# Up projections of three networks as seven block products, with weight sums made partly by accumulating transfers

## The chip, the cores and the metric

One core of a Trainium2 chip runs the whole program. The time is device microseconds of one launch; before the change the median of three runs is 2175.71 us (2175.65 to 2176.05).

## The reference

Two transformer blocks follow each other on 512 tokens of width 1024, all in float32. Block one has a mixer (forgetting attention beside gated linear attention), a cross attention, and an MLP. Block two has a gated network (ffn1), a token mixer, a second gated network (ffn2) and a final norm. What the change touches is the three networks:

```python
# block one
u = relu(rms_norm(h, norm_mlp_g) @ mlp_w1)        # 1024 -> 4096
h = h + (u * u) @ mlp_w2                          # 4096 -> 1024
# block two, twice (ffn1 and ffn2)
n = rmsnorm(x, g)
x = x + 0.5 * ((silu(n @ w1) * (n @ w3)) @ w2)    # 1024 -> 2816 twice, 2816 -> 1024
```

## The kernel before, in words

Activations lie with the features across the 128 partitions: `h` is 8 tiles (k) of 128 features by 512 tokens. Every float32 operand of a matrix product is split into a high part of the type that TensorE multiplies (fp32r) and a low part, the remainder. A product is then three matmuls, high by high, high by low and low by high (`product`, L557 to L559), added in one PSUM bank.

Weights come in panels of 1024 rows by 256 columns. SP issues their load into one of two `raw` buffers (`load`, L432, which waits on `conv_done`, so until VectorE has converted the panel before); ScalarE copies a panel to `wh` (`conv` of its block, L1365), VectorE subtracts to `wl` (`conv`, L2114), and TensorE runs it in `panel_t`: for each of the two 128-column halves c, 8 tiles k by 3 matmuls of 512 tokens, 48 in all, into the bank `lin0` or `lin1`. A down panel over six k tiles has 36. `begin(p, c)` makes TensorE wait until VectorE has emptied that bank of the panel before, and `pe.wait_ge(conv_done, p + 1)` until the panel is converted. Each engine works through its own instructions in the written order.

A network is cut into chunks. A chunk has its up panels first and then four down panels whose result VectorE adds to `h` (`residual`). The MLP has four chunks of 4 up and 4 down panels. ffn1 and ffn2 have two chunks of 8 up panels (w1 and w3 in turns) and 4 down, then one of 6 up panels and 4 down panels of six k tiles. The up products are made from the features without the token's norm factor; VectorE multiplies the factor `N_rs` in afterwards. The MLP does VectorE relu by factor, ScalarE square and high part, VectorE low part. The gated one (`gated`) does VectorE factor, ScalarE silu, VectorE factor and product, ScalarE high part, VectorE low part. The results stand in `ah`, `al` (in `xh`, `xl` for ffn2), from where `panel_t` takes them as the k tiles of the down panels.

GpSimd has no work beyond the start. The sub-blocks outside the networks keep their code.

Of the kernel before, what the change touches and what calls it, by code (L numbers as in the profile page):

```python
# [11 lines left out]
PART = 128  # L12
# [26 lines left out]
for name_, count_ in (("small", 1), ("fqk", 4), ("fv", 2), ("gqk", 2), ("gv", 2), ("gr", 2), ("xk", 4), ("xv", 4),  # L39
                      ("wout", 4), ("xq", 4), ("xo", 4), ("mlp", 32), ("ffn1", 34),  # L40
                      ("mix2", 32), ("mnsa", 8), ("wout2", 4), ("ffn2", 34)):
    P0[name_] = at
    at += count_
# [59 lines left out]
MLP0 = {"mlp": 2, "ffn1": 2 + 32, "ffn2": 2 + 32 + 22}  # L103
ML_S0 = MLP0["ffn1"]

# [69 lines left out]
def build(nc, d, out):  # L175
    ctx = ExitStack()
    with ctx:
# [8 lines left out]
        xh = sb("xh", [PART, KT, T], F32R)  # L186
        xl = sb("xl", [PART, KT, T], F32R)
        ah = sb("ah", [PART, KT, T], F32R)
        al = sb("al", [PART, KT, T], F32R)
        raw = sb("raw", [PART, 2, KT, PC])  # L190
# [19 lines left out]
        AW = 16360  # L210
# [55 lines left out]
        sm_done, sm_z = sem("sm_done"), sem("sm_z")  # L266
# [26 lines left out]
        e_half, e_add, e_sq, e_ac = sem("e_half"), sem("e_add"), sem("e_sq"), sem("e_ac")  # L293
        out_c = [sem("out_c" + str(t)) for t in range(QT)]
# [59 lines left out]
        E_t, E_u = A(2, T), A(2, T)  # L354
# [45 lines left out]
        def landed(p):  # L400

            return 16 * (p // 2 + 1)

# [4 lines left out]
        def _(sp):  # L408
# [60 lines left out]
            for r in range(0, D_FF // D):  # L469
                for j in range(4):  # L470
                    load(r * 8 + (P0["mlp"] + j), (P0["mlp"] + j) % 2, mw1[:, :, bass.ds(r * D + j * PC, PC)])
                for j in range(4):
                    load(r * 8 + (P0["mlp"] + 4 + j), (P0["mlp"] + j) % 2, mw2[:, bass.ds(r * KT, KT), j * PC:(j + 1) * PC])

            def ffn(name):
                w1, w3, w2 = ffw[name]
                p0 = P0[name]
                for r in range(0, 2):
                    for j in range(4):
                        for e, w in enumerate((w1, w3)):  # L480
                            load(r * 12 + (p0 + 2 * j + e), (p0 + e) % 2, w[:, :, bass.ds(r * D + j * PC, PC)])
                    for j in range(4):
                        load(r * 12 + (p0 + 8 + j), (p0 + j) % 2, w2[:, bass.ds(r * KT, KT), j * PC:(j + 1) * PC])
                for j in range(3):
                    for e, w in enumerate((w1, w3)):
                        load(p0 + 24 + 2 * j + e, (p0 + e) % 2, w[:, :, 2 * D + j * PC:2 * D + (j + 1) * PC])
# [2598 lines left out]
```

## Time and profile before

| | before |
|---|---|
| median of three runs | 2175.71 us |
| span of the profiled execution | 2174.4 us |
| TensorE busy | 2157.7 us, 99% |
| VectorE busy | 1144.9 us, 53% |
| ScalarE busy | 904.4 us, 42% |
| GpSimd busy | 0.2 us |
| transferred | 199.45 MB, mean 92 GB/s |

The span runs from the first to the last instruction of one profiled execution; the result gives no separate device time for that execution, so the median of the runs stands for it, 1.3 us above the span. "Busy" counts the time in which at least one instruction of an engine runs. Matmuls are pipelined and their ends are modelled: the distance between the starts of two neighbours says what one costs, not its duration.

### The profile page before, as it was taken

To read this page: it belongs to the slowest core of one execution; us is meant where nothing else is said; L and a number is where in the kernel's file an instruction comes from. 1 tells how busy PE (TensorE), PEld (TensorE's weight loads), DVE (VectorE), ACT (ScalarE), POOL (GpSimd) and SP (SyncE) were. 2 spreads that over 40 slices of the span, in tenths; PEclk is the share of its full clock that TensorE was granted. 3 is DMA by queue.
4 is the path that set the end of the run, shared out by engine and by line. 5 is a ranking of instruction groups with operands and counts; after the bars stand their busy time and mean duration, and the time that the engine had idled before them with its cause. 6 is when DMAs were issued, how large, how long until landed. Compare 5 with 4: busy or idle time off the path is not lost.

```text
span 2174.4 us, 28238 instructions
## 1 busy us (share of the span) xinstructions
PE 2157.7 (99%) x11510; PEld 1777.1 (82%) x11510; DVE 1144.9 (53%) x1985; ACT 904.4 (42%) x1526; POOL 0.2 (0%) x4
## 2 busy tenths in 40 slices
PE   9999999999999999999999999999999999999999
PEld 7888988888888888888888878887777888888887
DVE  4754664453433454344357677647776455434345
ACT  6654545442322332222234465546666233222224
POOL 0000000000000000000000000000000000000000
PEclk9999999999999999999999999999999999999999
DMA  5121521133333223323223622321111333333321
GB/s 186 59 78 59 194 97 59 59 95 99 97 94 99 94 90 98 104 87 107 86 90 95 199 80 82 98 83 49 45 30 40 97 97 97 98 97 97 98 87 68
DMA packets 190194, 199.45 MB, mean 92 GB/s; under 512 B 7777, under 2 KB 185074, under 8 KB 189554
## 3 DMA queue, kind: packets, MB, share of 16 engines
q1 hardware_dynamic: 190066, 197.66, 29.0%
q8 instruction: 91, 1.49, 0.3%
q14 instruction: 37, 0.30, 0.0%
HBM read 188.73 MB, written 2.10 MB: 88 GB/s over the span
## 4 chain that ended last, share of the span: by engine, by line
PE 97%; DVE 1%; ACT 1%; issue 1%; DMA 0%; SPq 0%; DVEq 0%; ACTq 0%
PE lin L557 28%; PE lin L559 27%; PE lin L558 27%; PE turned L658 3%; PE score L753 3%; PE mix L767 2%; PE mix L1201 1%; PE mix L1040 1%; PE score L1020 1%; PE score L869 1%; PE score L1252 0%; PE mix L1260 0%; PE score L1004 0%; PE mix L777 0%; DMA raw<-in_w_in_dram 0%
## 5 line engine op out<-in xcount | busy, mean ns | idle before, releaser
L557 PE MATMUL lin<-xh,wh 128*128 128x512 f32 (+1 forms) x1478 | 581.4, 393 | 1.7 <-DVE wl L2120 1.2
L559 PE MATMUL lin<-xh,wl 128*128 128x512 f32 (+1 forms) x1478 | 568.7, 385 | 0.0
L558 PE MATMUL lin<-xl,wh 128*128 128x512 f32 (+1 forms) x1478 | 567.6, 384 | 0.0
L557 PE MATMUL lin<-ah,wh 128*128 128x512 f32 x1044 | 407.8, 391 | 0.5 <-DVE h L2173 0.5
L559 PE MATMUL lin<-ah,wl 128*128 128x512 f32 x1044 | 405.5, 388 | 0.0
L558 PE MATMUL lin<-al,wh 128*128 128x512 f32 x1044 | 405.4, 388 | 0.0
L2114 DVE TENSOR_TENSOR wl<-raw,wh 128x2048 fp32r<-128x2048 f32 x129 | 295.7, 2292 | 185.1 <-ACT wh L1365 185.1
L1365 ACT ACTIVATE wh<-raw 128x2048 fp32r<-128x2048 f32 x129 | 245.8, 1906 | 263.6 <-PE lin L559 263.6
L557 PEld LDWEIGHTS lin<-xh,wh 128*128 128x128 f32 x1478 | 277.9, 188 | 63.1 <-issue 9.9
L559 PEld LDWEIGHTS lin<-xh,wl 128*128 128x128 f32 x1478 | 277.7, 188 | 56.5
L558 PEld LDWEIGHTS lin<-xl,wh 128*128 128x128 f32 x1478 | 278.2, 188 | 52.4 <-issue 1.0
L557 PEld LDWEIGHTS lin<-ah,wh 128*128 128x128 f32 x1044 | 196.0, 188 | 41.6 <-issue 0.9
L559 PEld LDWEIGHTS lin<-ah,wl 128*128 128x128 f32 x1044 | 196.0, 188 | 40.6
L558 PEld LDWEIGHTS lin<-al,wh 128*128 128x128 f32 x1044 | 196.1, 188 | 40.3 <-issue 0.2
L2120 DVE TENSOR_TENSOR wl<-raw,wh 128x1024 fp32r<-128x1024 f32 x90 | 109.6, 1221 | 40.2 <-ACT wh L1372 39.7
L2226 DVE CUSTOM_DVE_ANT_0 arena<-score,cst 128x128 f32<-128x128 f32 (+2 forms) x224 | 97.6, 487 | 57.9 <-PE score L753 46.7
L1462 ACT ACTIVATE arena<-arena,negm 128x128 f32<-128x128 f32 (+2 forms) x224 | 122.9, 555 | 3.0 <-DVE negm L2226 3.0
L2156 DVE TENSOR_TENSOR arena<-lin,N_rs 128x512 f32<-128x512 f32 x66 | 45.5, 689 | 139.5 <-PE lin L559 139.4
L1450 ACT ACTIVATE arena<-turned 128x512 f32<-128x512 f32 (+1 forms) x128 | 68.9, 582 | 112.4 <-PE turned L658 112.1
L1372 ACT ACTIVATE wh<-raw 128x1024 fp32r<-128x1024 f32 x90 | 94.2, 1053 | 35.6 <-PE lin L559 23.6
L1822 ACT ACTIVATE arena<-arena 128x512 f32<-128x512 f32 x44 | 27.8, 633 | 170.9 <-DVE arena L2156 170.9
L557 PE MATMUL lin<-wh,xh 128*128 128x256 f32 x320 | 92.5, 289 | 0.0
(349 smaller groups left out, 2120.8 us busy)
## 6 DMA issues: line engine op xcount, KB each, us to landing
raw<-in_ffn_w_dram SPq DMA_DIRECT2D x60, 1024.0 KB, 5.3
raw<-in_w_in_dram SPq DMA_DIRECT2D x38, 1024.0 KB, 5.3
raw<-in_mlp_w_dram SPq DMA_DIRECT2D x32, 1024.0 KB, 5.4
raw<-in_xattn_wkv_dram SPq DMA_DIRECT2D x8, 1024.0 KB, 5.5
raw<-in_w_out_dram SPq DMA_DIRECT2D x8, 1024.0 KB, 5.1
arena<-arena SPq DMA_DIRECT2D x104, 64.0 KB, 2.0
raw<-in_ffn_w_dram SPq DMA_DIRECT2D x8, 768.0 KB, 4.6
raw<-in_xattn_wq_dram SPq DMA_DIRECT2D x4, 1024.0 KB, 5.3
```

What stands on the lines that cost most here:

```text
L557: nc.tensor.matmul(o, w[0], x[0], start=first, stop=False)
L558: nc.tensor.matmul(o, w[0], x[1], start=False, stop=False)
L559: return nc.tensor.matmul(o, w[1], x[0], start=False, stop=last)
L658: mm = nc.tensor.transpose(pt[a][:, to:to + PART], PB[:, j % 2, a, lo:lo + PART], ident)
L753: mm = nc.tensor.matmul(ps[a][:, col:col + nk], q(piece, a, slice(t * PART, nk)), k(piece, a, nk), start=True, stop=True)
L1365: nc.scalar.activation(wh[:, p % 2], raw[:, p % 2], ACT.Copy).then_inc(hi_done, 1)
L1372: nc.scalar.activation(wh[:, p % 2, :, cols], raw[:, p % 2, :, cols], ACT.Copy).then_inc(hi_half[c], 1)
L1450: op = nc.scalar.activation(PTs[:, a, 0:w], pt[a][:, 0:w], ACT.Copy)
L1462: op = nc.scalar.activation(PB[:, s % 2, a, col:col + nk], SM[:, a, col:col + nk], ACT.Exp, bias=negm[:, at:at + 1], scale=-1.0, accum_out ...
L2114: nc.vector.tensor_tensor(wl[:, p % 2], raw[:, p % 2], wh[:, p % 2].bitcast(F32), ALU.subtract).then_inc(conv_done, 1)
L2120: nc.vector.tensor_tensor(wl[:, p % 2, :, cols], raw[:, p % 2, :, cols], wh[:, p % 2, :, cols].bitcast(F32), ALU.subtract).then_inc(conv_d ...
L2226: op = nc.vector.tensor_tensor_reduce(out=SM[:, a, col:col + nk], in0=ps[a][:, col:col + nk], in1=mask, scale=scale, scalar=BIG, op0=ALU.a ...
```

## The change

A 2 by 2 block product by the Strassen-Winograd scheme replaces the plain one in all chunks but one of each network. For a pair of weight panels (`one`, `two`; in the gated networks w1 and w3 of the same columns) the weight blocks are A11, A12 (the upper and the lower four k tiles of `one`) and A21, A22 (those of `two`), each 4 tiles of 256 columns. The token blocks are the two halves of 256 tokens. Such a pair is a group: seven products (`PRODUCTS`), each of 2 by 4 by 3 = 24 matmuls of 256 tokens. The MLP has three phases of two groups, ffn1 and ffn2 two phases of four groups each, 22 groups in all, each phase followed by its four down panels as before.

Weight blocks: SP loads A21, A11, A12, A22 of a group, 512 KB each, into a buffer set: `raw`, or one that lies in `xl` (`al` for ffn2), in turns. S1 is A21 + A22: GpSimd issues a transfer that adds A22 from HBM to the loaded A21 (`add_22`). S2 = S1 + A11 and S4 = A12 + S2 are made by VectorE (`sum_2`, `sum_4`). S3 = A11 + A21 is again an adding transfer (`add_21`), issued once `sum_2` is done. Each of the seven blocks is converted by ScalarE and VectorE (`block_high`, `block_low`) into one of six slots (four half panels of `wh`, `wl`, two in `xh` or `ah`).

Token blocks: seven parts (`XS_h`, `XS_l`), made once per network, now with the norm factor multiplied in. They are made during the first chunk (`token_parts`, `token_parts_high`, `token_parts_low`), one quarter m at a time: in the gated networks quarters 0 and 1 behind its second and third pair of up panels, 2 and 3 between its down tiles. The chunk of 6 up panels and 36-matmul down panels now comes first instead of last.

Results: products share three PSUM banks per group. ScalarE copies a partial result out three times (`kept`) and VectorE adds or subtracts (`made_11`, `made_22`, `made_21`); the nonlinearity then runs on these tiles. Some semaphores at the end of the program are merged, and GpSimd's descriptor area is set to 2048.

The core of the diff:

```diff
+PRODUCTS = [(A11, B11, 0), (A12, B21, 2), (S2, T2, 0), (S3, T3, 1), (S1, T1, 0), (A22, T4, 1), (S4, B22, 0)]
...
+            def group_loads(g, p, free):
+
+                one, two = weights(g)
+                before = same_buffers(g)
+                for b, src in ((BZ, two[:, 0:HT]), (BP, one[:, 0:HT]), (BQ, one[:, HT:KT]), (BR, two[:, HT:KT])):
+                    if before:
+                        q = before[-1]
+                        if b == BZ:
+                            sp.wait_ge(st_a, sum_count(q, 2))
+                        else:
+                            sp.wait_ge(st_l, high_count(q, {BP: S3, BQ: S4, BR: A22}[b]))
+                    if buffers(g):
+                        sp.wait_ge(lin_done, 2 * free)
+                    else:
+                        sp.wait_ge(conv_done, p - 1 + b // 2)
+                    sp.dma_start(raw_of(g, b), src).then_inc((st_r, st_z, st_r, st_r)[b][buffers(g)], 16)
...
+            def add_21(g):
+
+                pool.wait_ge(st_a, sum_count(g, 1))
+                if g:
+                    pool.wait_ge(st_p, 16 * g)
+                pool.dma_start(raw_of(g, BP), weights(g)[1][:, 0:HT], accum_op=ALU.add).then_inc(st_p, 16)
...
+            def group(g):
+
+                (net, r), i = PHASE_OF[g]
+                for n, (a, b, at) in enumerate(PRODUCTS):
+                    o = banks(g)[at].rearrange("p (f n) -> p f n", f=2)
+                    (left_h, left_l) = parts_of(g, a)
+                    pe.wait_ge(st_l, high_count(g, a))
...
+                    if n in (2, 4, 5):
+                        pe.wait_ge(st_e, 3 * g + {2: 1, 4: 2, 5: 3}[n])
+                    elif n == 6:
+                        pe.wait_ge(st_c, 3 * g + 2)
+                    for c in range(2):
+                        cols = slice(c * PART, (c + 1) * PART)
+                        for k in range(HT):
+                            begins = n in (0, 1, 3) and c == 0 and k == 0
+                            nc.tensor.matmul(o[:, c, :], left_h[:, k, cols], XS_h[:, b, k, :], start=begins, stop=False, skip_group_check=True)
...
# scalar: a gated phase
+                for g in range(g0, g0 + n):
+                    more = g + 1 < g0 + n
+                    if g > g0:
+                        finish(g - 1)
+                    block_high(g, S3)
+                    if g > g0:
+                        high(g - 1, RIGHT, E_ur, gate_count(g, 0))
+                    kept(g, 0, (ml_e, 2 * MLP_G + gate_count(g, -1)))
+                    block_high(g, S4)
+                    if more:
+                        block_high(g + 1, A11)
+                    act.wait_ge(st_c, 3 * g + 1)
+                    nc.scalar.activation(E_tl, E_tl, ACT.Silu).then_inc(ml_s, 1)
+                    kept(g, 1, (ml_lo, made_count(g, -1)))
+                    if more:
+                        block_high(g + 1, A12)
+                    else:
+                        conv(p)
+                    kept(g, 2, (ml_lo, made_count(g, 0)))
+                    if more:
+                        block_high(g + 1, S1)
+                        block_high(g + 1, S2)
+                        block_high(g + 1, A22)
# vector: the token parts, a gated phase, the first chunk
+            def token_parts(name, gain, m):
+
+                if m:
+                    dve.wait_ge(st_l, part_count(name, m, 0))
+                for e in range(2):
+                    k = m + HT * e
+                    op = nc.vector.scalar_tensor_tensor(P_F[:, e, :], h[:, k, :], gcol(gain, k), N_rs[:], ALU.mult, ALU.mult)
+                op.then_inc(st_a, 1)
+                dve.wait_ge(st_a, token_count(name, m, 1))
+                nc.vector.tensor_tensor(P_T[:, T3 - T1, :], P_F[:, 0, RIGHT], P_F[:, 1, RIGHT], ALU.subtract).then_inc(st_a, 1)
...
+            def token_parts_low(name, m):
+
+                dve.wait_ge(st_h, part_count(name, m, 3))
+                low(XS_l[:, B11, m, :], P_F[:, 0, LEFT], XS_h[:, B11, m, :], st_l)
...
+                for g in range(g0, g0 + n):
+                    more = g + 1 < g0 + n
+                    if g > g0:
+                        finish(g - 1)
+                    block_low(g, S3)
+                    if g > g0:
+                        low_part(g - 1, RIGHT, E_ur, made_count(g, 0))
+                    block_low(g, S4)
+                    made_11(g)
+                    if more:
+                        block_low(g + 1, A11)
+                        block_low(g + 1, A12)
+                        block_low(g + 1, S1)
+                        sum_2(g + 1)
+                    else:
+                        conv(p)
+                    made_22(g)
+                    if more:
+                        block_low(g + 1, S2)
+                        sum_4(g + 1)
+                        block_low(g + 1, A22)
+                    made_21(g)
+                    gate(g, E_ul, E_tl, 3, gate_count(g, 1))
...
+                first = 4 if name == "mlp" else 5
+                residual(p, None, None, scale, 2, {0: third, 1: fourth, 2: fifth, first: early, first + 1: later})
+                last()
...
+                for j in range(TAIL):
+                    gated(p0 + 2 * j, m0 + 2 * j, j, dst, (lambda: token_parts_low(name, j - 2)) if j == 2 else None)
+                    if j:
+                        token_parts(name, own, j - 1)
+                token_parts_low(name, 1)
+                chunk(name, own, p0 + 6, 0.5)
+                ffn_phase(name, 1, dst)
+                rest(name, 2, 0.5)
+                ffn_phase(name, 2, dst)
+                residual(p0 + 14, after, gain, 0.5, 3 if after == "mix2" else 4)
```

`finish(g)` is, on ScalarE, the silu of `E_tr` and the high part of `E_ul`, on VectorE the low part of `E_ul` and the product of `E_ur` by `E_tr`. `third` is `token_parts` of quarter 2, `fourth` `token_parts_low` 2 and `token_parts` 3, `fifth` `token_parts_low` 3; `early` is the low parts of A11 and A12, `later` those of S1 and S2 with `sum_2` and `sum_4`, `last` that of A22. `token_parts` has two multiplications over 512 elements and four additions over 256, the first three in a chain; `token_parts_low` three subtractions over 256, 512 and 1024 elements. The MLP's phases are alike, with more instructions for square and parts; there the down panels' k tiles 4 to 7 wait for the last group (in ffn1 and ffn2 tiles 6 and 7).

In `residual` the pieces of `between[k]` stand behind the add of down tile k and ahead of the `conv` that follows tiles 1 and 3. ScalarE's order there is: high parts of token quarter 2, `conv` of the third down panel, high parts of quarter 3, `conv` of the fourth, and then the blocks A11, A12, S1, S2, A22 of the phase's first group, of which A11 waits until all of A11, A12 and A22 have landed. The blocks S3 and A22 of a first group go into slots that come free when the last down panel ends.

## Rows read from the trace of the kernel before

**Rows 1.** The page, parts 1 and 4: engine shares, and the chain that ended last.

```profile
PE 2157.7 (99%) x11510; PEld 1777.1 (82%) x11510; DVE 1144.9 (53%) x1985; ACT 904.4 (42%) x1526; POOL 0.2 (0%) x4
PE 97%; DVE 1%; ACT 1%; issue 1%; DMA 0%; SPq 0%; DVEq 0%; ACTq 0%
```

**Rows 2.** MLP, ffn1, ffn2: length, busy PE, PEld, DVE, ACT, POOL, clock, DMA, GB/s.

```profile
448.00:797.00 349.00, 349.00 (x1538) 288.43 (x1538) 151.22 (x144) 111.01 (x115) 0.00 (x0) 1.00 0.31 97
797.00:1164.00 367.00, 366.79 (x1619) 303.02 (x1618) 168.02 (x166) 105.11 (x100) 0.00 (x0) 1.00 0.29 93
1807.00:2161.00 354.00, 353.94 (x1562) 292.84 (x1563) 155.56 (x151) 99.69 (x94) 0.00 (x0) 1.00 0.28 89
```

**Rows 3.** Timeline of PE, first and last 512-token matmul of the MLP (1536).

```profile
448.40 0.79 PE L557 MATMUL lin<-xh,wh 128*128 128x512 f32 x1
...
796.78 0.39 PE L559 MATMUL lin<-xh,wl 128*128 128x512 f32 x1
```

**Rows 4.** Timeline of PE, a run of 264 matmuls of 256 columns, and its stretch.

```profile
235.06 0.36 PE L557 MATMUL lin<-xh,wh 128*128 128x256 f32 x1
...
266.69 0.28 PE L559 MATMUL lin<-wh,xl 128*128 128x256 f32 x1
235.06:266.70 31.64, 31.64 (x267) 1.00 0.69 233
```

**Rows 5.** Costliest groups by shape, VectorE: busy, mean ns of one.

```profile
L2114 DVE TENSOR_TENSOR wl<-raw,wh 128x2048 fp32r<-128x2048 f32 x129 | 295.7, 2292 | 185.1 <-ACT wh L1365 185.1
L2120 DVE TENSOR_TENSOR wl<-raw,wh 128x1024 fp32r<-128x1024 f32 x90 | 109.6, 1221 | 40.2 <-ACT wh L1372 39.7
L2138 DVE SCALAR_TENSOR_TENSOR xl<-h,gT,xh 128x512 fp32r<-128x512 f32 x40 | 29.6, 751 | 27.7 <-ACT xh L1401 27.7
L2125 DVE TENSOR_TENSOR xl<-arena,xh 128x512 fp32r<-128x512 f32 x30 | 20.2, 686 | 1.2
L2475 DVE TENSOR_TENSOR h<-mix,h 64x256 f32<-64x256 f32 x16 | 6.1, 417 | 0.2
L2242 DVE TENSOR_SCALAR arena<-arena,coef 128x512 f32<-128x512 f32 x32 | 14.1, 484 | 0.6
L2242 DVE TENSOR_SCALAR arena<-arena,coef 128x128 f32<-128x128 f32 x32 | 7.7, 284 | 0.6
```

**Rows 6.** The same view for ScalarE.

```profile
L1365 ACT ACTIVATE wh<-raw 128x2048 fp32r<-128x2048 f32 x129 | 245.8, 1906 | 263.6 <-PE lin L559 263.6
L1372 ACT ACTIVATE wh<-raw 128x1024 fp32r<-128x1024 f32 x90 | 94.2, 1053 | 35.6 <-PE lin L559 23.6 <-DMA raw<-in_xattn_wkv_dram 4.5 <-DMA raw<-in_cmp_w_dram 3.7
L1812 ACT ACTIVATE ah<-arena 128x512 fp32r<-128x512 f32 x32 | 20.2, 632 | 1.0
L1383 ACT ACTIVATE arena<-lin 128x512 f32<-128x512 f32 x40 | 23.7, 592 | 42.2 <-PE lin L559 42.1
L1460 ACT ACTIVATE arena<-arena 128x256 f32<-128x256 f32 x8 | 3.1, 413 | 2.5 <-DVE arena L2936 2.5
```

**Rows 7.** Timelines of PE and DVE where ffn1's last down panels begin.

```profile
1122.07 0.39 PE L557 MATMUL lin<-ah,wh 128*128 128x512 f32 x1
...
1122.37 0.69 DVE L2640 TENSOR_TENSOR arena<-lin,arena 128x512 f32<-128x512 f32 x1 [4.75 <-PE lin L559]
...
1125.57 2.29 DVE L2114 TENSOR_TENSOR wl<-raw,wh 128x2048 fp32r<-128x2048 f32 x1 [1.11 <-ACT wh L1365]
1127.78 0.68 DVE L2175 SCALAR_TENSOR_TENSOR h<-lin,h 128x512 f32<-128x512 f32 x1
```

**Rows 8.** The page, part 6: transfers, KB each, median us to landing.

```profile
raw<-in_mlp_w_dram SPq DMA_DIRECT2D x32, 1024.0 KB, 5.4
...
raw<-in_ffn_w_dram SPq DMA_DIRECT2D x8, 768.0 KB, 4.6
...
h<-in_x_t_dram SPq DMA_DIRECT2D x2, 1024.0 KB, 9.2
```

**Rows 9.** Waits of PE between 448 and 1160 us: the whole answer.

```profile
PE turned L607 <- DVE arena L2133: 0.4, 2, 0.2
```

More of the change, by code:

```diff
@@ new lines, in phase, with made @@
+            def phase(name, r, Y, panels=4):
+                g0, n, p = PHASES[name, r]
+                for g in range(g0, g0 + n):
+                    group(g)
+                def made(k):
+                    if name == "mlp":
+                        pe.wait_ge(ml_lo, made_count(g0 + k // 4, 4))
+                    else:
+                        pe.wait_ge(ml_lo, made_count(g0 + k // 2, 2))
+                for j in range(panels):
+                    panel_t(p + j, (p + j) % 2, Y, each=made if j == 0 else None)
@@ L1102, in _ @@
+                phase(name, 1, Y)
+                phase(name, 2, Y, 3 if name == "ffn2" else 4)
             ffn("ffn1", X, Y)
@@ new lines, in chunk, with third, fourth, fifth @@
+            def chunk(name, gain, p, scale):
+                early, later, last = first_blocks(PHASES[name, 1][0])
+                def third():
+                    token_parts(name, gain, 2)
+                def fourth():
+                    token_parts_low(name, 2)
+                    token_parts(name, gain, 3)
+                def fifth():
+                    token_parts_low(name, 3)
+                first = 4 if name == "mlp" else 5
+                residual(p, None, None, scale, 2, {0: third, 1: fourth, 2: fifth, first: early, first + 1: later})
+                last()
@@ new lines, in rest @@
+            def rest(name, r, scale):
+                early, later, last = first_blocks(PHASES[name, r][0])
+                first = 4 if name == "mlp" else 5
+                residual(PHASES[name, r][2] - 4, None, None, scale, 2, {first: early, first + 1: later})
+                last()
+            chunk("mlp", "norm_mlp_g", p + 4, 1.0)
+            for r in range(1, D_FF // D):
+                if r > 1:
+                    rest("mlp", r, 1.0)
+                mlp_phase(r)
+            residual(p + 16, "ffn1", "ffn1_norm_2")
@@ L2630, in gated @@
+            def gated(p, m, j, dst, between=None):
                 for c in range(2):
                     scaled(p, c, E_t[:, c, :])
+                if between:
+                    between()
                 for c in range(2):
```

538 lines of the change are left out of this document (425 added, 113 removed).

## The prediction

> **What bounds the kernel now.** I read the shares of the engines and the chain of waits first: TensorE is busy 99% of the span, and 97% of the chain that ended last is TensorE [rows 1]. Then the stretches of the three networks, 1070 us together: TensorE has no idle time there at the full granted clock (1.00, the 2.4 GHz level), VectorE is busy 43 to 46% and ScalarE 28 to 32% [rows 2]; TensorE's own waits over the first two of them come to 0.4 us [rows 9]. So work taken from TensorE counts in full there, and anything else counts only where it makes TensorE wait. The profiled execution's span is 2174.4 us, 1.3 below the median; I work on the span and add 1.3.
>
> **What TensorE saves.** The 1536 matmuls of the MLP start 348.38 us apart from first to last: 0.2270 us each [rows 3]. A pair of panels has 96: 21.79 us. A group has 7 x 24 = 168 matmuls of 256 columns. A run of 264 such matmuls, bank changes included, takes 31.63 us for 263 steps: 0.1203 us [rows 4], more than half of 0.2270, since some 13 ns of each are fixed. So a group takes 20.20 us, and the gain is 1.58 us, 7%, not the eighth that seven for eight suggests. 22 groups: 34.8 us. The other panels are the same ones in another order: nothing.
>
> **What is late in a gated group.** VectorE has 7 low parts and 2 sums of 1024 elements at 1.22, and 7 operations of 512 at 0.69: 15.8 of 20.2 us; ScalarE 7 x 1.05 + 3 x 0.59 + 4 x 0.63 = 11.7 [rows 5, 6]. In the MLP it is 17.2 and 14.2. That fits, so what counts is order. I laid the written orders out by hand from the row durations. Two corrections come from rows: back to back on an engine the next operation starts 0.08 us before the recorded end (a 2.29 conversion hands over after 2.21), and VectorE starts on a finished tile 0.30 us after TensorE's next start [rows 7]. With T the start of a group, products end every 2.89 us. The copy behind product 4 ends at T+12.4, S1 is converted high to 13.4 and low to 14.7, `sum_2` ends at 15.9. Then `add_21` runs; call its time from `sum_2` to landing X. In the next group (20.2 later) ScalarE has silu, high part, S3's high part, another high part and `kept(g, 0)` in this order, and TensorE's third product at +5.8 waits for that copy. S3's high part must therefore begin by +3.6: no wait while X is under 8.0. Above it each of the 12 such transitions loses X - 8.0. The 3 in the MLP behave nearly alike. S3's low part, `made_22` (done at 16.7 for product 7 at 17.3) and `add_22` (about 29 us early) are in time.
>
> **X.** No row has an adding transfer or one issued by GpSimd. Lower bound: 768 KB lands in 4.6 and 1024 KB in 5.4, so 512 KB in about 3.8. Upper bound: twice the 1024 KB row, 10.8; the slowest 1024 KB row has 9.2 [rows 8]. An add reads both operands, 1024 KB, so that row is the nearest; I take 6.5, the middle of 3.8 and 9.2, since the issuing path is untested. Rate is no limit: a group moves 3 MB in 20.2 us, some 156 GB/s, and the stretch of rows 4 ran at 233 with 69% of the engines [rows 4].
>
> The Trainium skill (Collectives: The Full Stack, on why a reduce-scatter is half of an all-gather) says that an add in a transfer costs two source reads and not its arithmetic. By it X would be the 1024 KB row, 5.4, and the time some 3 us lower than my forecast; no trace here shows an add.
>
> **The ffn's first chunk.** Here I expect TensorE to lose. A quarter's `token_parts` takes 2 x 0.75 and 4 x 0.42, partly overlapped: 3.1 us; `token_parts_low` 0.4 + 0.7 + 1.2, less overlaps, 2.1 [rows 5]. In front of down tile 0 stand the last low parts, the conversion of a down panel (ends at +5.7 after the down panels begin, as the trace shows at that place [rows 7]), `token_parts` 1 (to 8.8), ScalarE's high part of 1024 (to 9.9) and `token_parts_low` 1 (to 12.0). The add of tile 0 ends at 12.7. A down panel of 36 matmuls is 36 x 0.227 = 8.17 us, and the second one's first half needs that bank at 8.2: 4.5 us lost. Then `token_parts` 2, the add of tile 1, `token_parts_low` 2, `token_parts` 3 and a conversion come before the add of tile 2, which ends 12.1 us after tile 0's, where TensorE wants it 8.17 after: 4.0 lost. Two networks: 17.0 us. In the MLP the same pieces stand in panels of 10.9 us, and the critical adds end 1.5 us or more ahead of need: nothing.
>
> **The first group of a phase.** A11's high part waits for all three plain loads, and the last two are issued when the last down panel is converted. Behind the short down panels (phase 1 of ffn1, ffn2) that is 4.8 us after the third panel's start; they land at 10.3, A11 and A12 follow, S1 is low at 15.5, `sum_2` ends 0.4 after the phase begins, where 5.8 is the third product's mark: 5.8 - 0.4 - 1.6 (S3's high part and the copy) = 3.8. Two phases lose X - 3.8 = 2.7 each: 5.4 us. Behind whole down panels `sum_2` ends 2.1 before the phase: X - 6.3 = 0.2, two of them 0.4. In the MLP S1 is made one tile earlier: nothing up to 9.7.
>
> **The end of a phase.** MLP: relu, high, square, high and a low part run in series behind the last product, ending at 3.4, and k tile 4 wants them at 4 x 0.68 = 2.7: 0.7 x 3 = 2.1 us. Gated: 4.1 against tile 6 at 4.1: nothing.
>
> **The sum.** 34.8 - 17.0 - 5.4 - 0.4 - 2.1 = 9.9 us. Span 2164.5, time 2165.8. The range of X alone: at 3.8, 15.7 less (2160); at 5.4, 2163; at 8.0, 2171.8; at 9.2, the 15 transitions and 4 phase starts bring 2194; at 10.8, about 2228.
>
> **Rivals.** (1) *All hidden*: VectorE's insertions don't reach TensorE, because my hand order has errors of a few us at a place that comes only four times. For it: VectorE is 46% busy [rows 2]. Against: its order is fixed, and 8.17 us are to hold 12.1 us of its work between the adds of tiles 0 and 2. The time: 2175.7 - 34.8 + 2 = 2143; half hidden, 2153. (2) *The adding transfer is slow*, X over 8.5. It decides from 8.0 on, since S3's high part stands in ScalarE's order ahead of `kept(g, 0)`. At 9.2, 2194. For it: GpSimd issues nothing now, and 512 rows of 1 KB in two reads have no row here. (3) *Narrow matmuls cost more in place*: groups break even at 21.79 / 168 = 0.1297 us; at 0.125 the gain is 17 us, and the time 2183. Against: the 264 of rows 4 ran at 0.1203 with a semaphore wait every 24.
>
> The Trainium skill has a rule that speaks for (2): SBUF — State Buffer, the box on VectorE blocking transfers, says that a VectorE instruction in a two-port mode locks GpSimd out of writing descriptors; it measured a transfer of 0.62 us stretched to 3.1. That would make X about 9.
>
> As a mechanism of this kernel it would lengthen each add by a VectorE instruction or two. The rows show a fast mode only in L2242, 200 ns for 384 elements more (0.52 ns each); the conversions take 1071 ns for 1024 more (1.05 ns) [rows 5], and the phases have only such operations and products of two tensors. I give it 5%, inside (2).
>
> **Chances.** Forecast, X of 3.8 to 8.0 with the losses as worked out: 50%. (1), whole or half: 18%. (2): 22%. (3): 5%. Other losses of 5 to 10 us beyond mine: 5%. A measurement tells 0.2%, 4.4 us, from no change: same is 2171.4 to 2180.1. Faster is the forecast but for its upper edge, and (1): 69%; same is that edge, the start of (2), and small extra losses: 12%; slower the rest of (2) and (3): 19%. Range 2147 to 2190: it leaves out the wholly hidden case and X above 9. The forecast's own range is 2159 to 2172.
>
> **What would show it.** Matmuls of 256 columns at 0.120; a group 20.2 us apart from the next; TensorE waits before the second and the third down panel of ffn1's and ffn2's first chunk, 4 to 5 us each, ended by VectorE's add; X read as the gap from `sum_2`'s end to S3's high part; waits at the third product of a phase, ended by `kept`; VectorE about 78% busy in gated phases. I am wrong if TensorE runs through the first chunks without a gap, or if the third product of middle groups waits.

## The result and the profile after

The changed kernel takes 2179.13 us (median of 15 runs, 2176.01 to 2182.21), the kernel before 2175.95 (15 runs, 2175.62 to 2176.28): a ratio of 1.0015, 95% interval 1.0008 to 1.0022. It is 0.15% slower, clear of the noise, where the forecast was 0.45% faster (2165.8). The profiled execution took 2182.21 us with a span of 2180.4, so its span is 6.0 us longer than that of before, and it stands 3.1 above its median. Line numbers from here on are those of the changed kernel.

The page after, parts 1, 3 and 4, answers to [rows 1]:

```profile
PE 2130.9 (98%) x13100; PEld 1826.0 (84%) x13100; DVE 1325.2 (61%) x2237; ACT 1031.6 (47%) x1738; POOL 57.4 (3%) x48
q0 software_dynamic: 23232, 23.07, 7.1%
PE 84%; DVE 6%; DMA 4%; issue 3%; ACT 3%; SPq 0%; POOL 0%; DVEq 0%; ACTq 0%; POOLq 0%
```

TensorE's share of the chain that ended last fell from 97% to 84%. VectorE and transfers took the rest, although VectorE is busy only 61% of the span. The same three stretches as in [rows 2] (length, then busy PE, PEld, DVE, ACT, POOL, clock, DMA share, GB/s):

```profile
448.00:793.00 345.00, 340.38 (x1973) 299.46 (x1971) 209.35 (x228) 145.31 (x175) 15.73 (x12) 1.00 0.42 116
793.00:1160.00 367.00, 352.27 (x2172) 317.66 (x2171) 226.71 (x246) 150.54 (x175) 20.75 (x16) 0.98 0.45 116
1808.00:2164.00 356.00, 342.19 (x2121) 309.39 (x2120) 216.36 (x233) 145.81 (x170) 20.75 (x16) 0.98 0.44 113
```

In the gated networks TensorE now idles some 14 us in each, and the granted clock is 0.98 where it was 1.00. The waits of TensorE between 448 and 1160 us answer to [rows 9] (total, times, longest):

```profile
PE score L1281 <- ACT arena L2056: 10.4, 4, 8.3
PE lin L737 <- DVE h L2549: 6.3, 2, 4.5
PE lin L737 <- DVE al L2497: 1.8, 4, 0.6
```

The first row is the third product of a phase's first group waiting for the copy `kept(g, 0)`, the second the down panels of the first chunk waiting for the add of a down tile. Both are waits that the prediction named. The 8.3 is the one that it had as 2.7. In what follows a gap is the distance from the start of the matmul before it to the start of the one behind it, which is 0.1 to 0.2 us more than the wait.

**What the groups save.** Timeline of TensorE, where one group's product follows another by a whole group:

```profile
948.56 0.28 PE L1281 MATMUL score<-arena_r,wh 128*128 128x256 f32 x1
...
968.50 0.28 PE L1281 MATMUL mix<-arena_r,xh 128*128 128x256 f32 x1
```

168 matmuls in 19.94 us, 0.1187 each; [rows 4] had 0.1203. A group saves 21.79 - 19.94 = 1.85 us, and 22 of them 40.7.

In the same 19.94 us VectorE is busy 15.06 (76%; forecast 78%).

**What is lost.** I summed, over each network, how far every matmul's start lies behind its predecessor's beyond 0.227 us (512 columns) or 0.1185 (256 columns), less the same sum of the kernel before (0.8, 0.7, 0.1): 6.9 us in the MLP, 19.6 in ffn1, 20.7 in ffn2, 47.2 together. 40.7 less 47.2 is 6.5 us longer; the spans say 6.0. The lengths of the networks, from their first to their last matmul, say much the same: the MLP is 4.6 us shorter, ffn1 5.4 and ffn2 6.0 longer. By either way the split between places is good to about half a microsecond. The 47.2 by place: first chunk of both ffns 17.6, with another 1.5 of slower matmuls behind ffn2's; first group of their phase 1 20.4; MLP 6.9; small pieces 0.8.

**The first chunk.** Timelines of VectorE and ScalarE in ffn1, whose down panels begin at 855.88:

```profile
859.37 2.29 DVE L2486 TENSOR_TENSOR wl<-raw,wh 128x2048 fp32r<-128x2048 f32 x1 [1.12 <-ACT wh L1585]
861.58 1.41 DVE L2992 SCALAR_TENSOR_TENSOR arena<-h,gT,N_rs 128x512 f32<-128x512 f32 x2
...
864.74 1.06 ACT L2028 ACTIVATE arena_r<-arena 128x1024 fp32r<-128x1024 f32 x1 [0.77 <-DVE arena L3000]
865.83 2.16 DVE L2497 TENSOR_TENSOR arena_r<-arena,arena_r 128x256 fp32r<-128x256 f32 x3 [1.12 <-ACT arena_r L2028]
867.91 0.68 DVE L2549 SCALAR_TENSOR_TENSOR h<-lin,h 128x512 f32<-128x512 f32 x1
...
880.20 0.68 DVE L2549 SCALAR_TENSOR_TENSOR h<-lin,h 128x512 f32<-128x512 f32 x1
```

The conversion ends at +5.8 (forecast 5.7), the low parts at +12.1 (12.0), tile 0's add at +12.7 (12.7). The gap of TensorE runs from 863.81 to 868.73, 4.92 us. Tile 2's add begins 12.29 us after tile 0's (12.1). The second gap is only 2.15 us, since the 36 matmuls between the gaps took 10.15 us from the first start to the last instead of 7.95: the lower clock fell into a time that TensorE would have waited anyway.

**The first group of phase 1.** Timelines of GpSimd, VectorE and ScalarE in ffn1; the phase begins at 897.47, and the third product is wanted at 903.2:

```profile
884.88 1.29 POOL L714 DMA_DIRECT2D raw<-in_ffn_w_dram  x1 [162.42 <-DMA raw<-in_ffn_w_dram]
896.13 1.30 POOL L714 DMA_DIRECT2D xl_f<-in_ffn_w_dram  x1 [9.95 <-DMA xl_f<-in_ffn_w_dram]
902.90 1.29 POOL L721 DMA_DIRECT2D raw<-in_ffn_w_dram  x1 [5.47 <-DMA xl_f<-in_ffn_w_dram]
...
894.23 1.06 ACT L2049 ACTIVATE wh<-raw 128x1024 fp32r<-128x1024 f32 x1 [12.96 <-DMA raw<-in_ffn_w_dram]
...
899.46 1.23 DVE L3021 TENSOR_TENSOR raw<-raw 128x1024 f32<-128x1024 f32 x1
...
909.90 1.06 ACT L2049 ACTIVATE wh<-raw 128x1024 fp32r<-128x1024 f32 x1 [7.17 <-DMA raw<-in_ffn_w_dram]
910.86 0.58 ACT L2056 ACTIVATE arena<-score 128x512 f32<-128x512 f32 x1
...
911.59 0.55 PE L1281 MATMUL score<-arena_r,wh 128*128 128x256 f32 x1 [8.26 <-ACT arena L2056]
```

Four things are to be read. A11's conversion waited until 894.23 for a load; that put `sum_2` (L3021) at 899.46 to 900.69, 3.2 us into the phase instead of 0.4. `add_21` (L721) was not issued when `sum_2` ended but 2.2 us later, and its releaser is a transfer: the `add_22` issued at 896.13, which landed at 902.64. And it landed 6.98 us after its issue, at 909.88. The prediction's X, from the end of `sum_2` to the landing, was thus 9.2 here; in ffn2's first phase it was 9.6 (2.3 to the issue, 7.3 from there), in the second and third of the MLP 9.2 and 8.7. In the 15 groups that are not the first of a phase it was 6.2 to 6.6, once 7.7. Transfers of line L609 issued at 880.35 and 880.8 (the first two loads of the group), at 885.82 and 886.28 (its last two), and of L721 at 902.90, from issue to landing:

```profile
L609 SPq DMA_DIRECT2D raw<-in_ffn_w_dram x2: 368/410/452, 880.3 to 880.8; - x2
DMA to landing us min/median/max: 4.2/4.6/5.1
...
L609 SPq DMA_DIRECT2D raw<-in_ffn_w_dram x2: 367/416/465, 885.8 to 886.3; - x2
DMA to landing us min/median/max: 6.9/7.4/7.9
...
L721 POOL DMA_DIRECT2D raw<-in_ffn_w_dram x1: 1292/1292/1292, 902.9 to 902.9; - x1
DMA to landing us min/median/max: 7.0/7.0/7.0
```

The fourth is how full the transfer engines were. From 888 to 900 us:

```profile
888.00:900.00 12.00, 12.00 (x65) 10.37 (x64) 5.33 (x6) 2.96 (x3) 1.30 (x1) 1.00 1.12 308
```

Their share is 1.12 (the profile's count can pass 1) at 308 GB/s, where [rows 2] have 0.28 to 0.31 and [rows 4] 0.69 at 233, and the six loads issued from 885.8 to 890.7 landed one every 1.5 us, from 892.7 to 900.2.

Behind the gap TensorE ran at a lower granted clock, between its levels of 1.2 and 2.4 GHz on the mean (windows of 8 us):

```profile
912.00:920.00 8.00, 8.00 (x48) 8.00 (x48) 4.39 (x5) 3.51 (x5) 0.17 (x1) 0.65 0.98 245
920.00:928.00 8.00, 8.00 (x71) 8.00 (x70) 5.64 (x6) 3.67 (x4) 1.29 (x1) 1.00 0.22 39
```

48 matmuls where 71 go in the next 8 us. By the start-to-start sums this costs 2.8 us in ffn1 and 2.1 in ffn2. `add_21` over all 22 groups took 5.8 to 7.4 us from issue to landing, median 6.0; `add_22` took 5.7 to 8.9, median 6.6.

### The profile page after: what moved, and what is told of

Its sections match the earlier page's. It is cut to its first block, busy times and chain, and to the rows that moved or that the text cites. A ratio compares the mean times of both kernels' runs of the same rounds, so it can differ in the third digit from the quotient of the medians.

```text
span 2180.4 us, 32484 instructions
## 1 busy us (share of the span) xinstructions
PE 2130.9 (98%) x13100; PEld 1826.0 (84%) x13100; DVE 1325.2 (61%) x2237; ACT 1031.6 (47%) x1738; POOL 57.4 (3%) x48
## 4 chain that ended last, share of the span: by engine, by line
PE 84%; DVE 6%; DMA 4%; issue 3%; ACT 3%; SPq 0%; POOL 0%; DVEq 0%; ACTq 0%; POOLq 0%
PE lin L737 18%; PE lin L739 17%; PE lin L738 17%; PE mix L1281 3%; PE mix L1283 3%; PE mix L1282 3%; PE turned L838 3%; PE score L933 3%; PE score L1281 2%; DMA raw<-in_ffn_w_dram 2%; PE score L1283 2%; PE score L1282 2%; PE mix L947 2%; DMA raw<-in_mlp_w_dram 1%; DVE wl L2486 1%
## 5 line engine op out<-in xcount | busy, mean ns | idle before, releaser
L737 PE MATMUL lin<-xh,wh 128*128 128x512 f32 (+1 forms) x1032 | 409.5, 397 | 8.6 <-DVE h L2549 6.8
L739 PE MATMUL lin<-xh,wl 128*128 128x512 f32 (+1 forms) x1032 | 396.1, 384 | 0.0
L738 PE MATMUL lin<-xl,wh 128*128 128x512 f32 (+1 forms) x1032 | 395.2, 383 | 0.0
L737 PE MATMUL lin<-ah,wh 128*128 128x512 f32 (+1 forms) x788 | 310.3, 394 | 8.8 <-DVE h L2549 6.3
L739 PE MATMUL lin<-ah,wl 128*128 128x512 f32 (+1 forms) x788 | 306.9, 389 | 0.0
L738 PE MATMUL lin<-al,wh 128*128 128x512 f32 (+1 forms) x788 | 306.8, 389 | 0.0
L2486 DVE TENSOR_TENSOR wl<-raw,wh 128x2048 fp32r<-128x2048 f32 x85 | 194.8, 2291 | 142.2 <-ACT wh L1585 142.2
L1585 ACT ACTIVATE wh<-raw 128x2048 fp32r<-128x2048 f32 x85 | 161.9, 1905 | 99.6 <-PE lin L739 90.3
L1281 PE MATMUL score<-arena_r,wh 128*128 128x256 f32 x416 | 119.5, 287 | 17.5 <-ACT arena L2056 17.4
L1282 PE MATMUL score<-arena_r,wh 128*128 128x256 f32 x416 | 118.9, 286 | 0.0
L1283 PE MATMUL score<-arena_r,wl 128*128 128x256 f32 x416 | 118.8, 286 | 0.0
```

Source lines behind the costliest of these rows:

```text
L737: nc.tensor.matmul(o, w[0], x[0], start=first, stop=False)
L738: nc.tensor.matmul(o, w[0], x[1], start=False, stop=False)
L739: return nc.tensor.matmul(o, w[1], x[0], start=False, stop=last)
L1281: nc.tensor.matmul(o[:, c, :], left_h[:, k, cols], XS_h[:, b, k, :], start=begins, stop=False, skip_group_check=True)
L1282: nc.tensor.matmul(o[:, c, :], left_h[:, k, cols], XS_l[:, b, k, :], start=False, stop=False, skip_group_check=True)
L1283: mm = nc.tensor.matmul(o[:, c, :], left_l[:, k, cols], XS_h[:, b, k, :], start=False, stop=k == HT - 1, skip_group_check=True)
```

## The experiments

The ratio of each is to the kernel before, run beside it (2175.7 to 2176.0 every time); "after" is the changed kernel as it stands (2179.13).

**e1_area: room for two adding transfers.** The area that the kernel sets aside for dynamic transfers is doubled; the working area gives up the bytes.

```diff
-        AW = 19936
+        AW = 19456
-    nc = _bacc.Bacc(..., dynamic_dma_scratch_size=2048)
+    nc = _bacc.Bacc(..., dynamic_dma_scratch_size=4096)
```

> The changed kernel with GpSimd's descriptor area at 4096 instead of 2048 (the arena 1.9 KB smaller, nothing else). Theory: with 2048 an adding transfer isn't issued until the one before it has landed; in the first group of a phase add_21 is issued 0.26 us behind add_22's landing, 2.2 us behind sum_2's end in ffn1. With room for two, add_21 is issued at sum_2's end: the gap ahead of the first phase's third product falls from 8.5 and 7.2 us to some 6.3 and 5.5, the one of 2.0 in the MLP shrinks, and the time falls by 4 to 6 us, to 2174. Rival: GpSimd is late for its own order or because transfers share the engines; then add_21 lands as late as now and the time stays at 2179.

2171.58 us (2169.61 to 2174.41, 10 runs), ratio to before 0.998 [0.997, 0.9989]. Timeline of GpSimd:

```profile
893.25 1.28 POOL L714 DMA_DIRECT2D xl_f<-in_ffn_w_dram  x1 [10.33 <-DMA xl_f<-in_ffn_w_dram]
898.04 1.28 POOL L721 DMA_DIRECT2D raw<-in_ffn_w_dram  x1 [3.50 <-DVE raw L3021]
```

The adding transfer is now released by `sum_2`, while `add_22` (landed 900.05) is still on its way. All 22 adding transfers at L721 are now issued 0.3 to 0.5 us after their `sum_2`; in after five of them came 1.9 to 2.5 us behind it. The gaps at the third products are 5.7 and 6.7 us instead of 8.5 and 7.2, and a gap of 2.0 us in the MLP (after's 624.54) is gone. The time is 7.5 us under after, so the wait for the area was real and cost about that. In ffn2 the gap fell by 0.6 only, although X fell from 9.6 to 6.5: `sum_2` ended 4.1 us into the phase instead of 1.5, since there were no 1.5 us of slow matmuls ahead of the phase to give the loads time, and the loads took 1.0 longer.

**e2_pool_order: the same wait attacked by order.** In a phase's first group GpSimd issues `add_21` ahead of the next group's `add_22`.

```diff
+                    if g == g0:
+                        add_21(g)
...
-                    add_21(g)
+                    if g > g0:
+                        add_21(g)
```

> The changed kernel with add_21 of a phase's first group issued ahead of add_22 of its second. Theory (GpSimd's queue holds add_21 back behind an add that is needed 20 us later): the same gain as with the larger area, 4 to 6 us, to 2174, and add_21 takes about 6 us instead of 7 since no other add runs beside it. Rival (sharing of the transfer engines by plain loads): add_21 takes as long from sum_2's end as before, and nothing is gained.

2183.73 us (2181.31 to 2184.03, 5 runs), ratio 1.0034 [1.0021, 1.0047]. TensorE's waits between 448 and 1160 us:

```profile
PE score L1284 <- ACT arena L2059: 4.8, 1, 4.8
PE mix L1284 <- ACT arena L2059: 4.0, 2, 3.0
```

The long wait shrank from 8.3 to 4.8, but the second group now waits for its own late `add_22` (gaps of 1.3, 3.3 and 3.0 us over the program). Issued first, `add_21` took 6.1 us in ffn1 as expected, but now the other one is late. While one such transfer has to wait for the other, either order makes one late; e1 takes the wait away with the order as it was.

**e3_late_loads: are the next group's loads in the way?** SP holds the second group's loads back until the first group's A12 is converted.

```diff
+                    if g == g0 + 1:
+                        sp.wait_ge(st_h, high_count(g0, A12))
```

> The changed kernel in which SP issues the four loads of a phase's second group only when A12 of the first has been converted high. Theory: these loads and add_22 share the transfer engines with the last two loads of the first group, which A11 waits for; they landed 6.9 and 7.9 us after issue where 5.4 was counted. Freed of them they land in about 5.5, A11 starts 2 us earlier and so does sum_2: the gap in front of the third product falls by about 2 us in ffn1 and ffn2, and add_22 of the second group comes later, behind add_21, which takes away its 2.2 us wait as well: 4 us each, 8 to 10 in all with the clock, 2170. Rival (the loads are late because the adding transfer itself hogs the engines): they still take 7 to 8 us and only the wait of add_21 goes.

2216.72 us (2215.49 to 2218.92, 4 runs), ratio 1.019 [1.0174, 1.0205]: the second group starves (waits of up to 12.8 us). What it was run for is the landing of the first group's last two loads, now with only `add_22` beside them (issue to landing):

```profile
L609 SPq DMA_DIRECT2D raw<-in_ffn_w_dram x2: 367/431/495, 902.7 to 903.2; - x2
DMA to landing us min/median/max: 6.4/6.8/7.3
```

Against 6.9 and 7.9 that is 0.5 to 0.6 us less. With nothing beside them the group's first two took 4.2 and 5.1, so `add_22` is the larger part of why the last two are late (2.2 us each) and the second group's loads the smaller.

**e4_tokens: the first chunk in another order.** The token parts of a quarter go into its up pair, so that at most one quarter's low parts stand in front of a down tile's add.

```diff
-                    gated(p0 + 2 * j, m0 + 2 * j, j, dst, (lambda: token_parts_low(name, j - 2)) if j == 2 else None)
-                    if j:
-                        token_parts(name, own, j - 1)
-                token_parts_low(name, 1)
+                    gated(p0 + 2 * j, m0 + 2 * j, j, dst, lambda: token_parts(name, own, j))
+                    if j < 2:
+                        token_parts_low(name, j)
```

> The changed kernel with the token parts of ffn1 and ffn2 moved: quarters 0, 1, 2 are made within up pairs 0, 1, 2 behind the two factor multiplications, their low parts behind the pair, the low parts of quarter 2 behind the add of down tile 0, and only quarter 3 between the down tiles. Theory (VectorE's written order costs TensorE 4.7 and 2.0 to 2.4 us before the second and third down panel of each first chunk): these four gaps go, with the slower clock behind them (about 1.7 us each): 14 to 17 us, to 2164. Rival (VectorE has too much work in the chunk, wherever it stands): gaps of the same sum appear at other down panels or at the up panels.

2159.16 us (2158.18 to 2163.27, 4 runs), ratio 0.9927 [0.9913, 0.9942]: 20.0 us under after. TensorE's waits in the same stretch keep the third products and have no `DVE h` row left:

```profile
PE score L1281 <- ACT arena L2056: 7.7, 2, 6.6
PE lin L737 <- DVE al L2495: 1.7, 4, 0.6
```

All four gaps of the chunks are gone. So the loss was order alone, not VectorE's load: the same instructions run. The waits at the third products and in the MLP are some 2.6 us shorter as well.

**e5_filler: the clock.** 56 idle matmuls stand in for most of the wait ahead of the third product.

```diff
+                    if n == 2 and i == 0 and r == 1 and net != "mlp":
+                        begin(PHASES[net, r][2], 0)
+                        for m in range(56):
+                            nc.tensor.matmul(pl[0][:, 0:PC], XS_h[:, 0, 0, 0:PART], XS_h[:, 1, 0, :], start=True, stop=True)
```

> The changed kernel with 56 idle matmuls of 256 columns into the free bank lin0 (result unused) in the place where TensorE waits longest, ahead of the third product of the first group of ffn1 and ffn2. They take 56 x 0.118 = 6.6 us of the 8.4 and 7.1 us that it waits there. Theory: the granted clock falls to its lower level in these two gaps and stays there for the first some 4 us of work behind each, which costs 2.8 and 2.1 us; kept busy, the engine resumes at the higher one: 5 us less, 2174. Rival: the slow stretch behind the gaps is caused by the transfers (the 16 engines are 97% busy there), not by the clock; then the time stays at 2179.

2179.3 us (2175.14 to 2183.12, 10 runs), ratio 1.0013 [1.0004, 1.0023]. The windows where after had 0.65:

```profile
912.00:920.00 8.00, 8.00 (x70) 8.00 (x70) 5.50 (x6) 4.40 (x6) 0.00 (x0) 1.00 1.01 257
```

The clock stays up when TensorE does not stand still, so the lower clock came from the gap and not from the transfers beside it (257 GB/s here too). On the time the experiment doesn't bear the theory out. The profiled run was 6.4 us shorter than after's, but the median, expected at 2174, is where after's is, although all ten runs have a higher mean clock (0.995 to 0.998) than any of after's 15 (0.991 to 0.994; part of that is the filled gap itself). The one profile is the second fastest of its ten runs and after's the slowest of its 15, so their difference says little, and what kept the median up is open. The cost of the lower clock below is thus a sum over one trace, not a difference of times.

**e6_no_add: a copy in place of the add.** The kernel leaves the additions out.

```diff
-                pool.dma_start(raw_of(g, BZ), weights(g)[1][:, HT:KT], accum_op=ALU.add)
+                pool.dma_start(raw_of(g, BZ), weights(g)[1][:, HT:KT])
```

(and the same at `add_21`)

> The changed kernel with GpSimd's transfers as plain copies: the addition is left out, so the weight blocks S1 and S3 hold A22 and A21 alone. Theory (an add costs its second read): add_21 from issue to landing falls from 6.0 us to the plain 512 KB figure of about 4, plus what GpSimd's own descriptor making takes: to 4.5 to 5; the gap ahead of a first phase's third product falls by about 2 x (add_22, add_21) to 4 and the time by 6 us or so, to 2173. Rival (the time is GpSimd's descriptor making, 1.3 us busy each, and the queue): add_21 stays at 5.5 or more and the time within 2 us of 2179.

2163.89 us (2162.53 to 2167.08, 4 runs), ratio 0.9946 [0.9931, 0.9961]. `add_21`'s place, the eight into `raw` in ffn1 and ffn2, with the issue to landing of all 22; then the first group's last two loads; then GpSimd's timeline there:

```profile
L721 POOL DMA_DIRECT2D raw<-in_ffn_w_dram x8: 748/750/760, 897.3 to 2067.7; - x8
DMA to landing us min/median/max: 3.9/4.2/5.2
...
L609 SPq DMA_DIRECT2D raw<-in_ffn_w_dram x2: 368/414/459, 883.1 to 883.6; - x2
DMA to landing us min/median/max: 5.1/6.0/7.0
...
892.52 0.75 POOL L714 DMA_DIRECT2D xl_f<-in_ffn_w_dram  x1 [9.93 <-DMA xl_f<-in_ffn_w_dram]
897.35 0.75 POOL L721 DMA_DIRECT2D raw<-in_ffn_w_dram  x1 [4.08 <-DVE raw L3021]
```

The add costs 1.8 us more than a copy (6.0 against 4.2) and 0.54 us of GpSimd more (1.29 against 0.75). Beside copies the last two loads land after 5.1 and 7.0 us instead of 6.9 and 7.9. The gaps are 3.1 and 3.3 us. The 15.2 us under after are more than the price of the add: with copies the small area holds nothing back. All 22 at L721 are issued 0.3 to 0.5 us after `sum_2`, in ffn1 0.4 us before the copy ahead has landed (897.78).

**c1_area_tokens: e1 and e4 together.**

> The changed kernel with both the larger descriptor area and the moved token parts. If the two losses are separate they add: 2179.1 - 7.5 - 20.0 = 2151.6, and the only waits over 1 us in the networks stand ahead of the third product of the first phases, 4 to 5 us each. If the first chunk's gaps had given the loads of the next phase time to land, the gain is less, 2155.

2151.51 us (2150.61 to 2152.57, 4 runs), ratio 0.9889 [0.9872, 0.9905]. That is 27.6 us under after; the two edits alone give 7.5 and 20.0, so they add up. It beats the kernel before and the changed one. What TensorE still waits for between 448 and 1160 us, and the two windows behind that wait:

```profile
PE score L1281 <- ACT arena L2056: 4.3, 1, 4.3
...
896.00:900.00 4.00, 4.00 (x22) 4.00 (x23) 3.49 (x4) 2.28 (x3) 1.30 (x1) 0.57 0.50 125
900.00:904.00 4.00, 4.00 (x37) 4.00 (x36) 1.23 (x1) 2.19 (x4) 0.00 (x0) 1.00 1.18 252
```

**c2_s1_first: S1 before A12, on top of c1.** A11 waits for the two loads that S1 needs, S1 and `sum_2` come before A12 in both orders.

```diff
-A11, A12, S1, S2, A22, S3, S4 = range(7)
+A11, S1, A12, S2, A22, S3, S4 = range(7)
...
-                if a in (A11, A12, A22):
-                    act.wait_ge(st_r[buffers(g)], 48 * len(same_buffers(g)) + 48)
+                if a == A11:
+                    act.wait_ge(st_z[buffers(g)], 32 * len(same_buffers(g)) + 32)
+                elif a in (A12, A22):
+                    act.wait_ge(st_r[buffers(g)], 32 * len(same_buffers(g)) + 32)
```

> The kernel with both, and S1 converted and sum_2 made ahead of A12 in every group, A11 waiting for its own load alone, and the slots given out anew to suit. Theory (the gap that is left at the first phases is the chain loads, S1, sum_2, add_21, S3): sum_2 starts 3 to 4 us earlier there, the gaps of 4 to 5 us fall to 1 or none, and the slow clock behind them goes: 2151.6 - 8 to 12 = 2140 to 2144. Rival: the new order makes another block late (A12 is now one place behind, conv(p) in the MLP behind kept), and the time stays at 2150.

2159.94 us (2158.82 to 2162.14, 4 runs), ratio 0.9927 [0.9912, 0.9942], 8.4 above c1. Timeline of GpSimd and `add_21`'s issue to landing in ffn1's first group:

```profile
890.72 1.28 POOL L714 DMA_DIRECT2D xl_f<-in_ffn_w_dram  x1 [11.67 <-DMA xl_f<-in_ffn_w_dram]
891.47 1.84 POOL L721 DMA_DIRECT2D raw<-in_ffn_w_dram  x1
...
DMA to landing us min/median/max: 9.3/9.3/9.3
```

The two adding transfers now start 0.75 us apart, and `add_21` takes 9.3 us instead of c1's 5.8. `sum_2` ended 2.8 us earlier against the phase than in c1 and bought nothing, because the transfer behind it met the other one and landed 2.0 later. Neither theory nor rival had this. Gaps of 6.5, 6.3 and, in the MLP, 2.4 us.

**c3_early_sum and e7_early_sum: the milder edit, with and without the larger area.** A11's wait as in c2, and S1's low part and `sum_2` one place earlier in the gated networks. c3 has it on top of c1, e7 on top of after.

```diff
+                    if gated_:
+                        block_low(g, S1)
+                        sum_2(g)
...
-                    block_low(g, S1)
-                    sum_2(g)
+                    if not gated_:
+                        block_low(g, S1)
+                        sum_2(g)
```

> The kernel with the larger area and the moved token parts, the order of the blocks as in the changed kernel, but A11 waiting for A11's and A21's loads alone, and, at the start of a gated phase, S1's low part and sum_2 ahead of the add of down tile 6. Theory (the gap of 4.5 us left at each first phase is the chain of loads, A11, A12, S1, sum_2, add_21): A11 starts 1.5 us earlier and one add of 0.7 leaves the chain, so sum_2 ends 2.0 to 2.4 us earlier and add_21 lands as much earlier; gaps 2.2 us each, and with the clock 2151.5 - 6 = 2145. Rival (an earlier add_21 only runs beside add_22 and the plain loads of the second group and takes 8 to 9 us, as where S1 was put ahead of A12): add_21 lands at the same time and the median stays at 2150 to 2152.

> The changed kernel with only these last two edits (own load for A11, S1 and sum_2 earlier at the start of gated phases), descriptor area 2048 and token parts as in the changed kernel. Theory of the descriptor area: add_21 can't be issued before add_22 of the second group has landed, whenever sum_2 ends, so nothing is gained: 2178 to 2180. Rival (the late sum_2 is what sets the landing): 4 to 6 us less, 2174.

c3: 2153.23 us (2151.19 to 2155.58, 4 runs), ratio 0.9897 [0.9882, 0.9912], as c1: in ffn1 `sum_2` ends 0.8 us earlier against the phase, `add_21` takes 7.1 us instead of 5.8, and the gaps are 5.1 and 4.9 us (c1: 4.5 and 4.5). That is the rival's mechanism, smaller than the 8 to 9 us it gave `add_21`. e7: 2192.27 (2189.1 to 2193.1, 4 runs), ratio 1.0077 [1.006, 1.0094], 13 us above after. Timelines of GpSimd at the MLP's first phase, e7 and then c3:

```profile
529.32 1.31 POOL L714 DMA_DIRECT2D xl_f<-in_mlp_w_dram  x1 [10.82 <-DMA xl_f<-in_mlp_w_dram]
535.46 1.29 POOL L721 DMA_DIRECT2D raw<-in_mlp_w_dram  x1 [4.83 <-issue]
```

```profile
528.85 1.29 POOL L714 DMA_DIRECT2D xl_f<-in_mlp_w_dram  x1 [10.33 <-DMA xl_f<-in_mlp_w_dram]
530.70 1.28 POOL L721 DMA_DIRECT2D raw<-in_mlp_w_dram  x1 [0.56 <-DVE raw L3021]
```

e7 fits neither text: both expected 2174 to 2180. With the small area `add_21` is issued 0.25 us after `add_22`'s landing at 535.21, 4.6 us behind `sum_2`, and a gap of 3.9 us opens there (in after there is none over 0.6 at that place). With the larger one it goes 1.9 us behind `add_22`. In e7 the edit delays `add_22`, which now waits for two loads, and the small area passes the delay on. The gaps that differ from after's (2.5 us more in the MLP, 1.0 less in phase 1, 2.6 more in phase 2, 0.9 more in the first chunks) come to 5.0 of the 6.9 us by which its profiled span is the longer one. That span is from the fastest of its four runs and after's from the slowest of its 15, and what makes up the rest of the 13 stays open.

## Why the prediction was wrong

**The step that failed is "the first group of a phase"**, in the two places behind short down panels: 2.7 us each forecast, 8.4 and 7.1 measured as waits (gaps of 8.5 and 7.2), and 20.4 for 5.4 with the lower clock behind them, 15.0 too few. The other differences nearly cancel: the first chunks lost 2.1 more, the MLP 4.8 more, and the groups saved 5.9 more. Together they turn the -9.9 us of the forecast into the +6.0 of the spans (3.1 of which is how far this execution stood above its median). The prediction's sum for ffn1 was 0.4 + 6.5 + 1.6 - 5.8 = 2.7; with the measured values it is 3.2 + 9.2 + 1.6 - 5.7 = 8.3. The form of the sum holds; two of its terms were wrong, and a third cost had no term:
- "They land at 10.3": the last two loads were issued at 4.8 as forecast, but landed at 11.7 and 13.2. `sum_2` ended at 3.2 instead of 0.4: 2.8 us. The 5.4 of [rows 8] is a median of loads that run nearly alone; here `add_22` was issued 0.9 us before and four more loads from 0.6 us after. The last of a pair took 5.1 us alone, 7.3 with `add_22` beside it (e3) and 7.9 with the four loads too; with a copy for `add_22` and the four loads it took 7.0 (e6). "Rate is no limit" went with it: 156 GB/s is the mean over a group, but from 888 to 900 us the transfer engines' share was 1.12 at 308 GB/s.
- "Then `add_21` runs": it ran 2.2 us later, so X, which the prediction counts from `sum_2`'s end, was 9.2 and not 6.5. I had treated GpSimd's queue as order only, and missed that the area at the kernel's end (2048) bounds how many adding transfers are out. e1, and the pair c3 and e7, show it. From its issue the transfer took 7.0 us there, 0.5 more than the X forecast; over all 22 groups X was 6.4 in the median.
- The lower clock behind a gap was in no term: 2.8 and 2.1 us here, 1.5 behind ffn2's first chunk. The trace before holds no long gap in these stretches, so its rows could not price it.

In ffn2 the same sum is 1.5 + 9.6 + 1.6 - 5.7 = 7.0 for 7.1 measured: less from the loads, more from X.

**The other terms.** What TensorE saves: 34.8 forecast, 40.7 measured. The mechanism is right and the step is the mis-sized term, 0.1203 against 0.1187 a matmul: the run of [rows 4] is not the same code, and 1.3% of 168 matmuls is 0.27 us a group.

The first chunk: 17.0 forecast, 17.6 measured, and e4, which also shortens the later waits, returns 20.0. Right by each of its steps in ffn1; only the split over the two waits (4.5 and 4.0 forecast; 4.7 and 1.9 to 2.4 measured) is off, because the lower clock fell between them (2.2 and 1.7 us).

The MLP: 2.1 forecast, 6.9 measured. Its phase ends cost 0.54 to 0.56 each for the 0.7 forecast. 1.9 is a wait for `add_21` at 624.54, gone in e1: the prediction allowed X up to 9.7 there, but `sum_2` ended 3.3 us ahead of the phase and not 5.5, and X was 9.2. The rest is 0.7 or less in several places.

Gated middle groups: no wait forecast while X is under 8.0, no gap over 0.6 us found in any of the 12 transitions.

**The rivals.** That all is hidden is refuted. That the adding transfer is slow (X over 8.5) came true in part. From issue to landing none of the 22 `add_21` took over 7.4, and between two groups of a phase X never passed 7.7, so the cost that the rival put there did not come. But counted from `sum_2`'s end X was 8.7 to 9.6 in four of the seven first groups, through its late issue, and c2 shows 9.3 from issue to landing when two adding transfers overlap. The time lies in the wide range of 2147 to 2190, outside the forecast's own of 2159 to 2172. Narrow matmuls are cheaper in place, not dearer.

The Trainium skill's rule on reads (Collectives: The Full Stack, why a reduce-scatter is half of an all-gather) gave an estimate of 5.4 for X. The runs show 6.0 from issue to landing beside a copy's 4.2: the add is dearer than a copy, as the rule has it, and 0.6 above the price that I drew from it. The Trainium skill's rule on VectorE's port (SBUF — State Buffer, the box on VectorE blocking transfers) gave an estimate near 9; GpSimd was busy 1.29 to 1.31 us with 43 of the 44 adding transfers and 1.44 with the first, with VectorE busy 61%, so the trace shows no lock-out of that size.

## What to carry to other kernels

When a change adds transfers from a queue that was idle, price three things by themselves: its length, what it does to the loads that are due beside it, and how many of its kind can be out at once. Neither a load's median over the program nor a mean rate over 20 us is a price for the one place where several are issued within 2 us of each other. By the start-to-start sums a stop of 4 to 8 us on TensorE cost 1.5 to 2.8 us more than its length here (the one test by the time, e5, did not confirm it), and an engine at 61% held TensorE up where its order puts 12 us of work between two adds that are wanted 8 us apart: moving that work gave 20 us, and with the larger area this kernel went from 0.15% slower to 1.1% faster.

## What the runs showed of the hardware

- A 512 KB adding transfer issued by GpSimd: 6.0 us from issue to landing at `add_21` (5.8 to 7.4), 6.6 at `add_22` (5.7 to 8.9), and 1.29 us of GpSimd; the same as a copy 4.2 (3.9 to 5.2), 5.1 (3.9 to 6.6) and 0.75. Two adding ones 0.75 us apart: 9.3 us for the second.
- With 2048 set aside for dynamic transfers the second adding transfer is issued 0.25 us after the first has landed; with 4096 it goes while the first is out. A second copy goes while the first is out with 2048 too (e6).
- Two 512 KB loads issued 0.5 us apart by SP: 4.2 and 5.1 us alone, 6.4 and 7.3 with an adding transfer out, 6.9 and 7.9 with four more loads behind them; under that load one landed every 1.5 us.
- Behind a stop of 4.5 us the granted clock was 0.57 on the mean over the next 4 us (22 matmuls of 256 columns for 37), and behind one of 8.5 us 0.65 over 8 us. With idle matmuls in the stop it stayed at 1.00.
- Matmuls of 256 columns in the groups start 0.1187 us apart, those of 512 columns 0.2270.
